# Token rows of the next expert job by indirect DMA, tiles in pairs at phase starts, DMA issues moved from ACT to SP

## The reference

```python
h = rmsnorm(x, lp["norm1"]) * (1 + sc1) + sh1
u = h @ lp["w_in"]
...
merged = gates[:, :, 0] * y_conv + gates[:, :, 1] * y_fno + gates[:, :, 2] * y_rwkv
x = x + g1 * (merged @ lp["w_o"])
h = rmsnorm(x, lp["norm2"]) * (1 + sc2) + sh2
x = x + g2 * ffn(h)
```

```python
logits = (t @ w_router).astype(jnp.float32) + b_router.astype(jnp.float32)
top_v, top_i = lax.top_k(logits, TOP_K)
top_p = jax.nn.softmax(top_v, axis=-1)
comb = jnp.sum(jax.nn.one_hot(top_i, N_EXPERTS, dtype=jnp.float32) * top_p[..., None], axis=1)
for e in range(N_EXPERTS):
    y = y + comb[:, e:e + 1].astype(t.dtype) * swiglu(t, w_gate[e], w_up[e], w_down[e])
```

## Time and profile before

| | us |
|---|---|
| median of 3 runs | 1898.19 (1896.22 to 1906.67) |
| the profiled execution | 1911.24 |
| its span | 1909.3 |
| of the span: up to the experts' loop | 1377.0 |
| the experts' loop, 9 jobs | 505.0 |

### The profile page before, as it was taken

The page is one execution under the profiler, slowest core; times in us unless marked ns, Lnnn a source line. Parts: engine busy times, 40 slices in busy tenths (PEclk is TensorE's granted clock), DMA queues, the critical chain, the costliest instruction groups (busy, mean ns, idle before and its releaser), DMA issues.

```text
span 1909.3 us, 40982 instructions
## 1 busy us (share of the span) xinstructions
PE 1778.1 (93%) x16558; PEld 1628.1 (85%) x16558; DVE 1130.6 (59%) x1623; ACT 902.9 (47%) x1358; POOL 556.3 (29%) x423
## 2 busy tenths in 40 slices
PE   7898989899999999989988899999899999999996
PEld 6896868799999999989968788999788878888885
DVE  2365688754331111033666885532589888889987
ACT  3335242243344333333441423434567777777765
POOL 1560000265566666656600003656300000000000
PEclk9998989999999999989999999999999999999998
DMA  8446141233423444423571101336388999899880
GB/s 286 153 135 225 48 130 60 82 117 116 154 78 122 133 133 133 125 86 106 162 229 60 33 4 32 111 127 217 133 312 296 297 316 310 308 316 316 291 286 34
DMA packets 225286, 315.33 MB, mean 165 GB/s; under 512 B 15734, under 2 KB 169716, under 8 KB 225012
## 3 DMA queue, kind: packets, MB, share of 16 engines
q1 hardware_dynamic: 217856, 306.22, 48.8%
q10 hardware_dynamic: 7284, 6.97, 1.2%
HBM read 311.05 MB, written 2.10 MB: 164 GB/s over the span
## 4 chain that ended last, share of the span: by engine, by line
PE 78%; DVE 11%; issue 4%; ACT 4%; DMA 1%; ACTq 1%; DVEq 0%; POOL 0%; SPq 0%
PE bank L598 76%; PE bank L595 2%; DVE e_w_rest L186 2%; DVE S L1981 2%; DMA ring<-in_w_ada 1%; ACT e_w_rounded L1354 1%; DVE cvT L1884 1%; DVE hg_rest L1785 1%; DVE St L2033 0%; DVE U L2011 0%; DVE hT L1753 0%; DVE St L2030 0%; DVE hT L1734 0%; DVE tmp L1899 0%; DVE ey_rest L2291 0%
## 5 line engine op out<-in xcount | busy, mean ns | idle before, releaser
L2384 POOL TENSOR_TENSOR weights_rest<-ring,weights_rounded 128x512 fp32r<-128x512 f32 x344 | 467.4, 1362 | 457.7 <-ACT weights_rounded L1317 456.9
L186 DVE TENSOR_TENSOR e_w_rest<-e_raw,e_w_rounded 128x1024 fp32r<-128x1024 f32 (+1 forms) x326 | 353.7, 1132 | 35.0 <-ACT e_w_rounded L1354 33.8
L1317 ACT ACTIVATE weights_rounded<-ring 128x512 fp32r<-128x512 f32 x344 | 215.5, 629 | 335.1 <-PE bank L598 322.3
L1354 ACT ACTIVATE e_w_rounded<-e_raw 128x1024 fp32r<-128x1024 f32 (+1 forms) x327 | 315.2, 989 | 80.8 <-PE bank L598 80.2
L598 PE MATMUL bank<-h_rounded,weights_rounded 128*128 128x384 f32 x688 | 234.4, 341 | 12.4 <-DVE h_rest L1785 4.9
L598 PE MATMUL bank<-h_rest,weights_rounded 128*128 128x384 f32 x688 | 232.2, 338 | 0.0
L598 PE MATMUL bank<-h_rounded,weights_rest 128*128 128x384 f32 x688 | 232.2, 337 | 0.0
L598 PE MATMUL bank<-e_w_rounded,hG_rounded 128*128 128x512 f32 (+1 forms) x432 | 164.5, 381 | 6.7 <-DVE hG_rest L2283 3.5
L598 PE MATMUL bank<-e_w_rest,hG_rounded 128*128 128x512 f32 (+1 forms) x432 | 162.7, 377 | 0.0
L598 PE MATMUL bank<-e_w_rounded,hG_rest 128*128 128x512 f32 (+1 forms) x432 | 162.7, 377 | 0.0
L598 PEld LDWEIGHTS bank<-h_rounded,weights_rounded 128*128 128x128 f32 x688 | 131.1, 191 | 16.7 <-issue 6.0
(11 more groups left out here) (350 smaller groups left out, 3615.4 us busy)
## 6 DMA issues: line engine op xcount, KB each, us to landing
ring<-in_w_ada SPq DMA_DIRECT2D x96, 512.0 KB, 6.2
e_raw<-in_moe_w_down SPq DMA_DIRECT2D x90, 512.0 KB, 4.6
ring<-in_w_in SPq DMA_DIRECT2D x88, 512.0 KB, 4.5
e_raw<-in_moe_w_gate SPq DMA_DIRECT2D x72, 512.0 KB, 5.6
e_raw<-in_moe_w_up SPq DMA_DIRECT2D x72, 512.0 KB, 6.6
e_raw<-in_moe_w_gate SPq DMA_DIRECT2D x36, 384.0 KB, 3.8
e_raw<-in_moe_w_up SPq DMA_DIRECT2D x36, 384.0 KB, 3.9
ring<-in_ffn_w_gate SPq DMA_DIRECT2D x22, 512.0 KB, 4.6
```

Source lines behind the costliest of these rows:

```text
L186: eng.tensor_tensor(wl, e_raw[n % E_RAW][:, 0:kn * w], wr.bitcast(F32), ALU.subtract).then_inc(s("e_rest"), 1)
L1317: a(w_parts[n % NSLOT][0], raw, ACT.Copy).then_inc(*E.up("rounded_ready", *key))
L1354: a(e_w[n % E_PARTS][0][:, 0:kn * w], e_raw[n % E_RAW][:, 0:kn * w], ACT.Copy).then_inc(s("e_rounded"), 1)
L2384: pool.tensor_tensor(wl, raw, wr.bitcast(F32), ALU.subtract).then_inc(*E.up("rest_ready", *key))
```

## The change

**Rows by DMA.** POOL adds rounded part and rest of the tokens (`h_sums`, three additions of 128x1024) and stores them to DRAM (`h_rows`, 1.5 MB) at the start of the experts' stage. In each job one indirect DMA on POOL's queue brings the next job's 128 rows (512 KB) into `hgt`; the 12 gather matmuls and ACT's two copies stay only for job 0. The token numbers come with the slots' weights: `wsel` has a second column with the number of the token, and `slot_rows` makes both in bank 5, after piece 20, for the next job. DVE's select stands before the rest of piece 20, its new copies `slot_values` (row numbers and weights) behind the products of chunk 2. PE waits for these copies before piece 24 and for the rows before `turn_gathered`.

**Router.** DVE's steps for the weights go ahead of its wait for the ranks. The bias is added per expert before the logits are turned, so that `brt` is 8x1. DVE loads the number of jobs after hG's parts and two rests.

**Pairs of tiles.** `dense_two` makes the first two tiles of z, of the first gates, of o, and of fg and fu together: for each of the first two pairs of channel blocks the products of both tiles, then the second half of the first tile and that of the second. The pieces stand in that order (first halves of both, then second halves).

**DMA issues.** `second` is issued by SP before block 3 of z, and `st_in`, `wrt` and `brt` before block 5. `ahead` starts with the tile's own second piece, since it is no longer the next one, and ACT rounds a piece more before the opening's `modulate` and a piece of o at the end of the gates.

```diff
-        hT_parts = parts("htoken", DM, 3, o, o + 3 * DM); o += 6 * DM
+        hT_parts = parts("htoken", DM, 3, o, o + 3 * DM)
+        h_sums = cut("h_sums", o, 3 * DM).rearrange("p (j d) -> p j d", j=3)
+        hgt = cut("hgt", o + 3 * DM, DM); o += 6 * DM
...
-        hgt = cut("hgt", used["eprod"][0], DM)
+        hgt0 = cut("hgt0", used["eprod"][0], DM)
...
-        wsel = cut("wsel", o, 3); o += 3
+        wsel = cut("wsel", o, 6).rearrange("p (j w) -> p j w", w=2); o += 6
...
+        wnext = cut("wnext", o, 1); o += 1
+        rows_at = cut("rows_at", o, 1).bitcast(I32); o += 1
...
             for n, (key, (src, k, w), last) in enumerate(blocks):
+                if key == ("z", 0, 3, 0):
+                    sp.dma_start(second, dram["tables"][:, n_first:ncols]).then_inc(*S.up("second_in", by=16))
+                if key == ("z", 0, 5, 0):
+                    sti = st_in.rearrange("p (h k) -> p h k", h=NH)
+                    for d in range(2):
+                        sp.dma_start(sti[64 * d:64 * d + 64, :, :], dram["state_rwkv"][0, 0, d].rearrange("h v k -> v h k"))\
+                            .then_inc(*S.up("st_in", 0, by=16))
+                    sp.dma_start(wrt, dram["w_router"][0].rearrange("(k p) e -> p k e", p=P)).then_inc(*S.up("router_in", by=16))
+                    sp.dma_start(brt[0:NE, :], dram["b_router"].rearrange("o e -> e o")).then_inc(*S.up("router_in", by=16))
                 if key[0] == "z" and key[2:] == (4, 0):
...
-            def dense(job, phase, l, first=False):
+            def parts_wait(phase, l, g):
+                by_pool = (phase == "ffn" or phase == "z" and l > 0) and g % 2 == 0
+                pe.wait_ge(*at("x_parts_pool" if by_pool else "x_parts", phase, l, g))
+            def pair_products(b, key, phase, i):
+                w = w_parts[piece_at[key] % NSLOT]
+                for k in (4 * key[-1] + i, 4 * key[-1] + i + 1):
+                    last = three(b[:, 0:T], w, h_parts[phase], k % 4, k, k == 0, k == KD - 1)
+                return last
+            def dense(job, phase, l):
...
-                    w = w_parts[piece_at[key] % NSLOT]
-                    for i in range(4):
-                        k = 4 * half + i
-                        if first and k % 2 == 0:
-                            by_pool = (phase == "ffn" or phase == "z" and l > 0) and k % 4 == 0
-                            pe.wait_ge(*at("x_parts_pool" if by_pool else "x_parts", phase, l, k // 2))
-                        last = three(b[:, 0:T], w, h_parts[phase], i, k, k == 0, k == KD - 1)
+                    for i in (0, 2):
+                        last = pair_products(b, key, phase, i)
...
+            def dense_two(jobs_, phase, l):
+                banks = [begin(*job) for job in jobs_]
+                for i in (0, 2):
+                    parts_wait(phase, l, i // 2)
+                    for job, b in zip(jobs_, banks):
+                        if i == 0:
+                            pe.wait_ge(*at("rest_ready", *job, 0))
+                        last = pair_products(b, job + (0,), phase, i)
+                        if i == 2:
+                            last.then_inc(*E.up("piece_used", *job, 0))
+                for job, b in zip(jobs_, banks):
+                    pe.wait_ge(*at("rest_ready", *job, 1))
+                    for i in (0, 2):
+                        if job == jobs_[0]:
+                            parts_wait(phase, l, 2 + i // 2)
+                        last = pair_products(b, job + (1,), phase, i)
+                    last.then_inc(*E.fill(*job))
...
-                        dense(("gate", l, BRANCHES[pos], m), "gate", l, pos == 0 and m == 0)
+                        if pos == 0 and m == 0:
+                            dense_two([("gate", l, BRANCHES[0], m_) for m_ in range(2)], "gate", l)
+                        elif pos > 0 or m > 1:
+                            dense(("gate", l, BRANCHES[pos], m), "gate", l)
...
-            def turn_gathered(i):
+            def turn_gathered(first):
...
-                    pe.wait_ge(s("e_hgt"), i * 2 + h + 1)
+                    if first:
+                        pe.wait_ge(s("e_hgt"), h + 1)
...
-                        last = transpose(psum[h][:, k * P:(k + 1) * P], hgt[:, (4 * h + k) * P:(4 * h + k + 1) * P])
+                        last = transpose(psum[h][:, k * P:(k + 1) * P], (hgt0 if first else hgt)[:, (4 * h + k) * P:(4 * h + k + 1) * P])
...
-                    transpose(psum[4][:, j * P:(j + 1) * P], sel[:, j, :].bitcast(F32))
+                    last = transpose(psum[4][:, j * P:(j + 1) * P], sel[:, j, :].bitcast(F32))
+                last.then_inc(s("e_selT_full"), 1)
+            def slot_rows(i):
+                pe.wait_ge(s("e_wsel"), i + 1)
...
-                    last = mm(psum[5][:, 0:1], sel[:, j, :].bitcast(F32), wsel[:, j:j + 1], j == 0, j == 2)
-                last.then_inc(s("e_selT_full"), 1)
+                    last = mm(psum[5][:, 0:2], sel[:, j, :].bitcast(F32), wsel[:, j, :], j == 0, j == 2)
+                last.then_inc(s("e_slot_full"), 1)
...
                             scatter(i, SCATTER_AT.index(n))
+                        if n == SLOTS_AT:
+                            slot_rows(i + 1)
                     if c == 1:
...
                         pe.wait_ge(s("e_selT"), i * 2 + 2)
+                        pe.wait_ge(s("e_rows_at"), i + 2)
                     if k0 == DOWN[1][0]:
...
                     e_piece(i, n, eprodT, lambda k, c0: (psum[4 + (E_PIECES[n][3] + c0) // 512], k == 0, k == KE - 1))
-                    if n == GATHER_AT:
-                        pe.wait_ge(s("e_sel"), i + 2)
-                        for h in range(2):
-                            for part in range(2):
-                                gather(h, part)
-                    elif n == GATHERED_AT:
-                        turn_gathered(i + 1)
+                    if n == GATHERED_AT:
+                        pe.wait_ge(s("e_rows_in"), i * 16 + 16)
+                        turn_gathered(False)
             pe.wait_ge(s("e_hG"), njobs * 2 + 2)
...
+                    convert(1)
...
-                    modulate(l, 0, between=convert)
-                    act.dma_start(second, dram["tables"][:, n_first:ncols]).then_inc(*E.up("second_in", by=16))
-                    act.dma_start(wrt, dram["w_router"][0].rearrange("(k p) e -> p k e", p=P)).then_inc(*E.up("router_in", by=16))
-                    act.dma_start(brt, dram["b_router"].broadcast_to([P, NE])).then_inc(*E.up("router_in", by=16))
-                    load_state(0)
+                    modulate(l, 0, between=lambda: convert(2))
...
                         a(selT, psum[4][:, 0:3 * P].rearrange("p (j s) -> p j s", j=3), ACT.Copy).then_inc(s("e_selT"), 1)
-                        a(wslot, psum[5][:, 0:1], ACT.Copy).then_inc(s("e_selT"), 1)
+                        act.wait_ge(s("e_rows_at"), i + 1)
+                        a(wslot, wnext, ACT.Copy).then_inc(s("e_selT"), 1)
                     if c > 0:
...
                 e_turn(2)
-                e_round(i, done + 4, GATHER_AT + E_PARTS)
-                e_gathered(i + 1)
-                e_round(i, GATHER_AT + E_PARTS, GATHERED_AT + E_PARTS)
+                e_round(i, done + 4, GATHERED_AT + E_PARTS)
                 e_hG_round(i + 1)
...
+            def select_weights(code):
+                for j in range(3):
+                    ins = dve.tensor_copy(wsel[:, j, 0:1], rt[:, code(R_CW + 24 * j)])
+                return ins
+            for i in range(2):
+                dve.wait_ge(*at("weights_ready", i))
+            for i in range(2):
...
+            dve.wait_ge(*E.latest())
+            first_, second_ = (rt[:, R_OH + 24 * i:R_OH + 24 * i + 24].rearrange("p (j t e) -> p j t e", j=3, t=1)
+                               .broadcast_to([P, 3, 3, NE]) for i in range(2))
+            tt(by_slot(R_CW), first_, second_, A).then_inc(*E.step())
+            dve.wait_ge(*E.latest())
+            dve.tensor_copy(wsel[:, :, 1], tab("token")[:, 0:3]).then_inc(*E.step())
+            select_weights(lambda at_: slice(at_, at_ + 1)).then_inc(s("e_wsel"), 1)
...
-                return ins
-            def select_weights(code):
-                for j in range(3):
-                    ins = dve.tensor_copy(wsel[:, j:j + 1], rt[:, code(R_CW + 24 * j)])
...
-            select_weights(lambda at_: slice(at_, at_ + 1))
...
+            njobs = dve.value_load(rt_i[0:1, 0:1], min_val=NE, max_val=NJOB)
+            def slot_values(i):
+                dve.wait_ge(s("e_slot_full"), i + 1)
+                dve.tensor_copy(rows_at, psum[5][:, 1:2])
+                dve.tensor_copy(wnext, psum[5][:, 0:1]).then_inc(s("e_rows_at"), 1)
+            slot_values(0)
...
                         add_output(i, n_)
+                    if c == 2:
+                        e_rests(i, done, SELECT_AT)
+                        dve.wait_ge(s("e_selT_full"), i + 1)
```

(37 more changed lines are left out.)

87 lines of the change are left out of this document (47 added, 40 removed).

## The result

| | median us | runs |
|---|---|---|
| before | 1906.32 (1896.22 to 1916.68) | 16 |
| after | 1916.19 (1910.60 to 1928.95) | 16 |

The changed kernel takes 1.0052 times as long (95% interval 1.0032 to 1.0072), 9.9 us more. The forecast was 0.5 us less, and 1897.7 as the time. That time started from before's median of 1898.19 in 3 runs; in these 16 runs, timed beside the changed kernel, before takes 1906.32. The profiled execution of after has a span of 1918.5 us, that of before 1909.3; both lie 4 to 5 us above their medians.

The account below looks back on a forecast made before the run. PE was taken as the bound, with 78% of the chain of waits. Phase starts −21.0, router +3, nine jobs +4 and clock +13.5 gave −0.5 on the median of 1898.19: 1897.7 us, range 1879 to 1914.

Parts of the forecast that it names:

- A plain stretch of dense tiles (600 to 640): Dense tiles: PE busy for all 40 us, 233 matmuls at 0.172 us each, so little idle time to win.
- Opening −9.8: Opening: tiles in pairs and issues gone from ACT let 55 matmuls end at 56.4 instead of 66.2, gain 9.8 us.
- FFN, z, gates: −11.2: Phase starts: pairs of tiles gain 3.3 us at layer 0's FFN, 3.3 at layer 1's z, 2.3 at each gates.
- Router and first job +3: Experts' start: shorter router path against POOL's additions slowing DVE's first rests and PE's small matmuls, +3 us (0 to +6).
- PE's wait +3.15: Each job, before piece 24: PE waits for DVE's copies of the slot values, +3.15 us (2 to 3.6).
- The job's sum of +0.44: One loop job: removed gathers, added wait, moved select and a saved small wait sum to +0.44 us; nine jobs +4.
- The clock, 1.5 a job: Loop: low clock after PE's idle wait costs 1.5 us in each of nine jobs, +13.5 (0 to +15).
- Rival A: Loop: the clock stays up despite the waits, sum −14.0, 1884 us; chance 0.27.
- The rows by DMA: Each job: the 512 KB by index has 11.5 us before the turning after piece 31; hidden, cost 0.
- Rival B: After piece 31: rows land late and PE waits; at 14 us, +22 us, 1920; chance 0.15.
- Rival C: Opening: moved DMAs on SP delay a weight block by 10 us, the 9.8 gain goes, 1907 us; chance 0.08.
- D: Before piece 24: PE's wait is much shorter, half of it and no clock falls, 1870 us; chance 0.05.

Follow-up runs that it names:

- x2: The kernel before with four unused columns behind the first tables, so everything behind them stands 16 bytes further on; 1915.20 us, ratio 1.0050 to before.
- x3: The changed kernel with DVE's copies of the slot values moved ahead of the rest of piece 24; 1874.51 us, ratio 0.9854 to before.
- x4: The changed kernel with four unused columns behind the first tables and the slot values' copies ahead of piece 24's rest; 1861.88 us, ratio 0.9793 to before.
- x6: The kernel before with only the slots of the dense weights' parts and what stands behind them moved by 16 bytes; 1910.00 us, ratio 1.0037 to before.
- x8: x1 with the opening's five DMA issues back on ACT, brt still 8x1; 1918.42 us, ratio 1.0081 to before.
- x10: x1 without tiles in pairs: the first two tiles of each phase one after the other; 1922.05 us, ratio 1.0113 to before.
- x9: x4 with POOL's three additions begun only when the list of jobs is ready; 1864.71 us, ratio 0.9812 to before.
- x7: The changed kernel with 12 useless matmuls of 512 columns ahead of PE's wait for the slot values; 1901.40 us, ratio 0.9999 to before.
- x1: The changed kernel with four unused columns behind the first tables, everything behind back at multiples of 32 bytes; 1906.71 us, ratio 1.0031 to before.

## Why the prediction was wrong

The time was forecast at 1897.7 and measured at 1916.19, 18.5 us more and 2 above the upper end of the range. Two steps of the prediction failed.

**The first is the one that said least.** "A plain stretch of dense tiles (600 to 640) is busy for all of its 40 us with 233 matmuls, 0.172 us each" was taken over to the kernel after: every stretch that the diff does not name stood in the sum at nothing. The change was forecast at −0.5 us and measured at +9.9, and most of these 10.4 lie there. There are 4,500 matmuls of 384 columns in the dense tiles and the small products, each some 2 ns slower, which makes 9 us, of which 7.6 stand in the balance above. x2 and the pair of x3 and x4 show that cause alone (a ratio of 1.0050 onto the kernel before; 12.6 us between x3 and x4). The line of the diff that does it adds the token table to the first tables; it was read for what it computes and not for where it puts everything else.

**The second is the time that the sum was added to.** "The terms are differences of stretches which that execution shows like any other, so I take them from the median" took before's 1898.19 of 3 runs. Beside the changed kernel before took 1906.32 in 16 runs, 8.1 us more, and this is the rest of the 18.5. With that start the same sum gives 1905.8, and the range, moved with it, takes in what was measured. Nor does every execution show those stretches alike: the stop of 4.68 us in the opening was 2.06 and 2.45 in x2 and x6.

Point by point:
- Opening −9.8: measured −10.2 in the balance, but against the execution that the term was read from. Against x6 and x2 it is 7.0 and 4.9. That the size came out is in part luck. The larger part is the moved issues' (x8: 6.7 lost without them), and the pairs carry 2.1 (x10).
- FFN, z, gates: −11.2 forecast, −10.6 measured. The pairs are the mechanism at the gates (2.4 each by x10) and a part of it at the FFN and z (1.4 and 2.0 of 3.0 and 3.3).
- Router and first job +3: measured +4.2. The company of POOL's additions was named, its place was not: the forecast had 3.3 lost in the loop's first rests, the trace has 5.0 lost in two small steps of the router (2.33 and 2.99 us) and 1.4 in two rests (3.79 in place of 2.35). It was partly made up by the router's shorter path (1.14 us idle in x9, without the company, against 3.49 before).
- PE's wait +3.15: 3.09. The job's sum of +0.44 is confirmed by x7 (56.1 to 56.5).
- The clock, 1.5 a job with a fall in each: 1.6, in all nine. Rival A was wrong here.
- The rows by DMA: 7.1 us from issue to landing in the median, 11.5 were there. Rival B did not arise. By the Trainium skill ("DMA: Bandwidth & Descriptors", "Anatomy of one DMA — SWDGE (gpsimd) path") the estimate was 3.2 us; the measurement beside the expert loads is more than twice that.
- Rival C did not arise, and D not either: DVE was as late as forecast.

**What the change was worth** without its two flaws is x4: 1861.88 us, 0.9793 of before (0.9765 to 0.9820). Of the 54 us between it and after, x1 gives 9.5, x3 41.7; 51 together. By the ratios, which take out the drift of before, it is 49, of which x1 gives 4 and x3 38.

## What to carry to other kernels

A change that adds a few columns to an early buffer moves all that is laid out behind it, so compare the addresses of the operands as well as the order of the instructions, and compare matmul spacings in a stretch that the change doesn't touch. Where values that one engine makes early are copied by another, put the copy where the values are ready and not where the code of that stage ends. In this loop a wait of 3.1 us cost its own length and 1.6 us of low clock behind it; filling it with useless matmuls gave the 1.6 back, and doing the copy earlier gave both. A stop that is read from one execution should be looked up in a second one before it goes into a sum: the one in the opening was 4.68, 2.45 and 2.06 us with the same instructions.

## What the runs showed of the hardware

- In one stretch of the FFN, matmuls of 384 float32r columns at full clock follow each other every 173.0 ns with both operands at multiples of 32 bytes, 175.5 with both 16 bytes off, 179.6 with only the streamed one off, and 173.0 with only the loaded weights off. In the z tiles the last case is not free: 174.9 against 173.4. The expert matmuls of 512 columns, whose streamed operand stayed in line in all kernels while their loaded one (hG) moved with the rest, stood a median of 234 ns apart in before and 232 in after.
- PE idle for 3.09 us went with a fall of its clock from the higher to the lower level in all of nine jobs, about 1.5 us after PE went on in eight of them and during the wait in one; the same stretch filled with matmuls was followed by none.
- While POOL adds two operands of 128x1024 in 2.37 us, DVE's rests in SBUF, a step of 17 columns with one input and a cast of 16 columns end only after it (2.33 and 2.99 us in place of 0.17 and 0.18). Two operations of 128x512 that take one input from psum are not held (0.68 to 0.69 us each for all 20 in x9, the two beside the addition among them).
- How long a DMA issue holds its engine varies for one and the same instruction: the broadcast of 8 values of 4 bytes to 128 partitions took 4.94, 4.47 and 2.87 us in three executions, the load of the same 8 values to one partition each 1.63 to 2.32 in six.
